# A two-block model on one core: weights stored in load order by the host, modulation sums moved from TensorE and GpSimd to VectorE and ScalarE, nine expert loads issued inside the first block

## The reference, cut to what matters

```python
# first block
h = rms_norm(x, norm1_g)
q, ckv, qi, ki, wi, u, v, ga, gb = split(h @ w_in)           # 1024 -> 4296 columns
index = sum_h wi_h * relu(qi_h @ ki.T)                       # 8 indexer heads
sel = top 64 of the causal index for each token
scores = q_lat @ c_kv.T * scale + rel_bias[bucket(t - s)]    # on the selected keys
o = softmax(scores) @ c_kv ; y_a = (o @ w_uv) @ w_proj_a
y_b = (gelu(u) * (tril(w_spatial) @ layer_norm(gelu(v)) + b_spatial)) @ w_proj_b
x = x + (sigmoid(ga) * y_a + sigmoid(gb) * y_b) @ w_out
x = x + moe(rms_norm(x, norm2_g))    # 32 experts, 2 for each token; three 1 MB matrices each
x = rms_norm(x, final_norm_g)
# second block, two layers
for l in range(2):
    mod = silu(c) @ w_ada[l] + b_ada[l]                      # (1024) @ (1024 x 3072)
    shift, scale, gate = split(mod)
    h = rms_norm(x) * (1 + scale) + shift
    x = x + gate * (concat(rglru_branch(h), mlstm_branch(h)) @ w_out[l])
return rms_norm(x, final_g)
```

## Time and profile before

| what | us |
|---|---|
| runs | 1045.84, 1049.13, 1050.15 (median 1049.13) |
| the profiled execution, its own time | 1043.84 |
| its span in the trace | 1042.0 |
| TensorE busy | 954.0 (92%) |
| VectorE, ScalarE, GpSimd busy | 423.5, 266.7, 178.3 |
| data moved | 227.86 MB, mean 219 GB/s |

### The profile page before, as it was taken

The page is one execution under the profiler, slowest core; times in us unless marked ns, Lnnn a source line. Parts: engine busy times, 40 slices in busy tenths (PEclk is TensorE's granted clock), DMA queues, the critical chain, the costliest instruction groups (busy, mean ns, idle before and its releaser), DMA issues.

```text
span 1042.0 us, 14265 instructions
## 1 busy us (share of the span) xinstructions
PE 954.0 (92%) x5525; PEld 758.9 (73%) x5525; DVE 423.5 (41%) x923; ACT 266.7 (26%) x623; POOL 178.3 (17%) x158
## 2 busy tenths in 40 slices
PE   6999799999899978666799999999999999999997
PEld 6868577788766644334388888787888888878786
DVE  1469862147622211110452453554325246264422
ACT  3231222201311211011218243133011814413301
POOL 5949997601100000000200000000000000000011
PEclk9999899989889997888899999999999999999999
DMA  9947776448999999999834554232354445423211
GB/s 290 284 160 242 232 207 194 162 152 298 421 420 422 420 421 421 421 420 420 287 108 155 162 161 143 101 122 77 126 162 122 159 144 162 162 88 115 99 43 41
DMA packets 140962, 227.86 MB, mean 219 GB/s; under 512 B 8457, under 2 KB 126562, under 8 KB 128602
## 3 DMA queue, kind: packets, MB, share of 16 engines
q1 hardware_dynamic: 136632, 221.15, 59.6%
q0 software_dynamic: 1600, 4.35, 1.6%
q10 hardware_dynamic: 2658, 1.40, 0.4%
HBM read 225.81 MB, written 1.07 MB: 218 GB/s over the span
## 4 chain that ended last, share of the span: by engine, by line
PE 74%; SPq 10%; DVE 8%; DMA 3%; issue 2%; ACT 2%; ACTq 0%; DVEq 0%
PE bank L469 25%; PE bank L1104 10%; SPq L1141 9%; PE bank L956 5%; PE bank L934 5%; PE bank L711 3%; PE bank L805 3%; PE bank L976 3%; DMA s<-in_w_down 3%; PE bank L781 2%; PE bank L820 2%; PE bank L452 1%; PE bank L841 1%; PE bank L521 1%; PE bank L991 1%
## 5 line engine op out<-in xcount | busy, mean ns | idle before, releaser
L469 PE MATMUL bank<-hT,ring 128*128 128x256 f32 x1168 | 264.0, 384 | 0.2 <-ACT s L1256 0.2
L469 PEld LDWEIGHTS bank<-hT,ring 128*128 128x128 f32 x1168 | 221.4, 192 | 35.6 <-issue 5.8
L1104 PE MATMUL bank<-ring,s 128*128 128x256 f32 x512 | 111.2, 379 | 0.0
L1104 PEld LDWEIGHTS bank<-ring,s 128*128 128x128 f32 x512 | 97.1, 190 | 13.1
L2214 POOL DMA_DIRECT2D s<-in_final_g x1 | 0.6, 604 | 472.8 <-DVE s L2057 472.8
L805 PE MATMUL bank<-s,z 128*32 128x256 f32 (+1 forms) x544 | 63.5, 415 | 8.8 <-DMA s<-in_w_up 6.4
L1832 DVE SCALAR_TENSOR_TENSOR z<-z,bank 128x256 f32<-128x256 f32 x9 | 3.8, 421 | 161.1 <-ACT z L1356 160.9
L2155 POOL TENSOR_TENSOR ring<-ring,csil 128x2048 f32<-128x2048 f32 x17 | 61.4, 3610 | 12.7 <-PE bank L495 11.7
L956 PE MATMUL bank<-ring,hT 128*128 128x256 f32 x256 | 56.6, 380 | 0.0
L934 PE MATMUL bank<-hT,ring 128*128 128x256 f32 x256 | 55.6, 379 | 0.0
L956 PEld LDWEIGHTS bank<-ring,hT 128*128 128x128 f32 x256 | 48.3, 190 | 7.7 <-issue 1.3
(11 more groups left out here) (413 smaller groups left out, 1490.9 us busy)
## 6 DMA issues: line engine op xcount, KB each, us to landing
ring<-in_w_in SPq DMA_DIRECT2D x56, 1024.0 KB, 5.4
ring<-in_w_ada SPq DMA_DIRECT2D x24, 1024.0 KB, 6.2
ring<-in_w_out SPq DMA_DIRECT2D x20, 1024.0 KB, 4.9
s<-in_w_gate SPq DMA_DIRECT2D x18, 1024.0 KB, 20.7
s<-in_w_up SPq DMA_DIRECT2D x16, 1024.0 KB, 22.1
ring<-in_w_down SPq DMA_DIRECT2D x12, 1024.0 KB, 23.6
s<-in_w_down SPq DMA_DIRECT2D x12, 1024.0 KB, 26.9
ring<-in_w_gate SPq DMA_DIRECT2D x10, 1024.0 KB, 25.6
```

What stands on the lines that cost most here:

```text
L469: mm = pe.matmul(b[:, 0:T], w[:, (k0 + kb) * CW + m * P:(k0 + kb) * CW + (m + 1) * P], rhs[:, kb, :], start=(kb == 0), stop=(kb == nk - 1))
L1104: mm = pe.matmul(xo[j, tt][:, 0:CW], yT[:, kb, tt * P:(tt + 1) * P], w[:, kb, :], start=(kh == 0 and kb == 0), stop=(kh == 1 and kb == KB ...
```

## The change

- The host now writes every piece of the two blocks in the order in which it is loaded, 8 KB for each partition, so a load is one contiguous 1 MB read. It also gives x turned (`x_T`), the small vectors as columns, the bias by distance and the spatial weights turned.
- `w_ada` pieces are stored with the output column on the partition and the 1024 inputs along the free axis, twice (two halves of 1024). One instruction with an accumulated output, 128x1024, does half a piece: VectorE does both halves of 18 pieces. For six pieces GpSimd does the 128x2048 multiplication alone, and ScalarE copies the two halves with accumulation. The 24 small TensorE jobs and the ScalarE copies of 2 columns go.
- The start: ScalarE and VectorE square x_T, TensorE sums over the partitions with a matrix of ones (8 matmuls, after 12 warming ones), ScalarE takes the root, VectorE the reciprocal of 128x256 and then writes the eight blocks of hT.
- The index weights come with the latent piece; the index key is written twice by two 64-column matmuls for each block. `cT` is turned between the two q pieces. The causal mask of the index is added by VectorE with `tri`.
- The bias of a head is added to the mask on VectorE ahead of the scores (`masked_bias`), and the matmuls with `anti` go. Two gate jobs stand ahead of the attention loop, and rounds 5 to 8 have one gate job instead of two.
- The biases of the spatial product are added on VectorE.
- Merged buffers: gmT in guT, oaT in w4, mgT in tga. So s6, s7 and vaug are dead in the whole first block. The first nine expert loads are issued behind pieces 14, 18, 22, 41 to 45 and 48; slots are used in another order.

The diff, cut to its core:

```diff
+GATES_FIRST, GATES_TWICE = 2, 5
+WARM_START = 12
-ADA_LAG = 2
-ADA_POOL = 17
+ADA_LAG = 1
+ADA_FIRST, ADA_POOL = 2, 6
+EARLY_LOADS = (14, 18, 22, 41, 42, 43, 44, 45, 48)
...
-        moe_slots = [RING + i for i in range(8)] + [(NB1 + i) % RING for i in range(RING)] + \
-            [RING + 8 + i for i in range(4)]
+        moe_slots = [RING + i for i in (7, 8, 6, 0, 2, 3, 1, 4, 5)] + [(NB1 + i) % RING for i in range(RING)] + \
+            [RING + i for i in (9, 10, 11)]
...
-                    for m in range(2):
-                        mm = pe.matmul(b[:, m:m + 1], adasum[:, n % 3, m * P:(m + 1) * P], allone[:, 0:1],
-                                       start=True, stop=True)
...
+            for _ in range(WARM_START):
+                pe.matmul(psum[0][:, 0:P], allone[:, :], allone[:, :], start=True, stop=True)
+            b = B.acquire(pe, "ssq")
             for kb in range(KB):
-                for tt in range(TT):
-                    m = pe.matmul(b[:, tt * P:(tt + 1) * P], x[:, tt, kb * P:(kb + 1) * P], rdiag[:, tt, :],
-                                  start=True, stop=True)
+                pe.wait_ge(S["sq_v" if kb // 2 % 2 else "sq_a"], 2 * (kb // 4) + kb % 2 + 1)
+                mm = pe.matmul(b[:, 0:T], allone[:, :], sqT[:, kb, :], start=(kb == 0), stop=(kb == KB - 1))
...
+            for _ in range(GATES_FIRST):
+                gate_job()
             for h in range(HEADS + 1):
...
-                        pe.matmul(b[:, 0:ns], anti[:, :], biasT[:, h, T - ns:T], start=True, stop=False)
...
-                gate_job()
+                if h < GATES_TWICE:
+                    gate_job()
...
-                    pe.matmul(b[:, c * P:(c + 1) * P], ones[0:1, :], bsp[0:1, g * P:(g + 1) * P], start=True, stop=False)
...
         def _(sp):
+            for n in range(NB1):
+                load(n, a["first_pieces"][n])
+                if n == RING - 1:
+                    sp.dma_start(x[:, :, :], ...)
+                if n in EARLY_LOADS:
+                    load_expert(len(early))
+                    early.append(n)
...
         def _(act):
+                if ADA_FIRST <= n < ADA_FIRST + ADA_POOL:
+                    act.wait_ge(S["ada_scaled"], n + 1 - ADA_FIRST)
+                    step(f(w[:, 0:D], w[:, 0:D], ACT.Copy, scale=0.5, accum_out=adac[:, l, 2 * j:2 * j + 1]))
+                    step(f(w[:, D:2 * D], w[:, D:2 * D], ACT.Copy, scale=0.5, accum_out=adac[:, l, 2 * j + 1:2 * j + 2]),
+                         S["ada_summed"])
...
         def _(v):
+            step(v.reciprocal(rbc, rbc))
+            for kb in range(KB):
+                step(stt(hT[:, kb, :], xT[:, kb, :], colA[:, kb:kb + 1], rbc, ALU.mult, ALU.mult), S["hT_ready"])
+            def ada_sums(count):
+                for n in range(ada["n"], ada["n"] + count):
+                    v.wait_ge(slot_full[c % RING], fill_value[c])
+                    step(stt(w[:, 0:D], w[:, 0:D], 0.5, csb, ALU.mult, ALU.mult, accum_out=adac[:, l, 2 * j:2 * j + 1]))
+                    step(stt(w[:, D:2 * D], w[:, D:2 * D], 0.5, csb, ALU.mult, ALU.mult,
+                             accum_out=adac[:, l, 2 * j + 1:2 * j + 2]), S["ada_summed_v"])
...
+            def masked_bias(h):
+                for tt in range(TT):
+                    step(tten(sc[:, tt, 0:ns], bias[:, h, T - ns:T], maskb[:, tt, 0:ns], ALU.add))
...
-                step(tten(gmT[:, g, :], b[:, 0:T], guT[:, g, :], ALU.mult), B.free)
+                step(tten(gsum, b[:, 0:T].rearrange("p (c t) -> p c t", c=TT),
+                          bsp[:, g, :].unsqueeze(1).broadcast_to([P, TT, P]), ALU.add))
+                step(tten(gmT[:, g, :], gsum.rearrange("p c t -> p (c t)"), guT[:, g, :], ALU.mult), B.free)
...
         def _(g):
-                    step(g.tensor_tensor(w, w, csil[:, :].unsqueeze(2).broadcast_to([P, KB, CW]), ALU.mult))
-                    step(g.tensor_tensor(w[:, 0:4, :], w[:, 0:4, :], w[:, 4:8, :], ALU.add))
-                    step(g.tensor_tensor(w[:, 0:2, :], w[:, 0:2, :], w[:, 2:4, :], ALU.add))
-                    step(g.tensor_tensor(adasum[:, n % 3, :], w[:, 0, :], w[:, 1, :], ALU.add), S["ada_summed"])
+                    step(g.tensor_tensor(w, w, csb.unsqueeze(1).broadcast_to([P, 2, D]), ALU.mult), S["ada_scaled"])
...
+def piece(w, tag):
+    if kind == "in":
+        t = by_column(w["w_in"][0], at[0])
...
+    elif kind == "ada":
+        l, j = at
+        t = w["w_ada_2"][l][:, j * CW:(j + 1) * CW].T.reshape(2, P, D).transpose(1, 0, 2)
```

562 lines of the change are left out of this document (233 added, 329 removed).

## The result

The changed kernel takes 1022.37 us, median of 4 runs (1020.47 to 1025.11), against 1049.62 for the kernel before (1045.84 to 1050.15): a ratio of 0.975 with a 95% interval of 0.972 to 0.978. It is faster, by 27 us where I forecast 49, and outside the range of 984 to 1019. The profiled execution took 1021.64 us, its span is 1019.9.

The account below looks back on a forecast made before the run. TensorE was taken to bound the first block, then the expert load stream; stage gains summing to 36.9 us put the experts at 254.6 and the last landing at 454.4, span 996.5, forecast 1000 us, range 984 to 1019.

Parts of the forecast that it names:

- q and index: Query and index stage: two modulation jobs go, gain 0.7 us; VectorE's wait cancels against the existing wait for the engines.
- rival D: First block: VectorE becomes the bound throughout, slower than before; 1060 at 9 us a modulation piece; chance 0.02.
- Rival B: Loads collide before the experts, TensorE waits for pieces, index stage may lose 5 to VectorE's start: 1018 us; chance 0.08.
- C: First block: fewer stalls than counted at V, the start's clock, q and index, and attention: 988 us; chance 0.17.
- Attention: Attention heads: bias matmuls and a job go (10.4 us), waits and slow clock too (8.1): gain 18.5.
- Start: Start to first qi projection: qi begins at 11.8 instead of 14.34, a gain of 2.5 us.
- cT, K, V: Small vectors, bias and cT: 4.6 us go, 2.5 come back through ScalarE's modulation copies ahead of K's: gain 2.1.
- Output projections: Output projections: four jobs go (1.4 us) and the first row runs at full clock (2.5).
- The stream: Expert loads: from the 19th issue at 258.4, 1.8 us start-up and 78 loads at 2.49; last lands at 454.4.
- the pairs of 64 columns side by side: Latent piece: doubled index-key matmuls of 64 columns run side by side at no cost; one after the other, 3.5 more.
- the spatial products: Spatial products: eight bias matmuls go (3.3 us), VectorE's second instruction shows with 0.7: gain 2.6.
- Rival A: VectorE's accumulating instruction runs at half pace, 4.7 us a modulation piece; experts begin 12 later: 1012 us; chance 0.15.

Follow-up runs that it names:

- e1: Changed kernel with each of GpSimd's six modulation multiplications shrunk to 8 of the 1024 columns of each half: 1010.64 us.
- e5: Changed kernel with GpSimd waiting for VectorE's last index sum before its first modulation multiplication, all work kept: 1018.07 us.
- e3: Changed kernel with ScalarE copying the previous head's transposed probabilities ahead of the two exponentials in attention rounds with one gate tile: 1016.87 us.
- e4: Changed kernel with ScalarE issuing the 512 KB broadcast load of c_2 only behind its squares: 1020.08 us.
- e10: Changed kernel with e3, e4, e6, all modulation sums on VectorE, seven throwaway matmuls before the first projection and x's load later: 1002.57 us.
- e6: Changed kernel with ScalarE's exponential of the recurrence parameters moved behind the copies of K and V: 1020.02 us.
- e11: Changed kernel with each of GpSimd's six modulation multiplications cut into four quarters of the columns: 1019.40 us.
- e7: Changed kernel with two more accumulating 128x1024 VectorE operations, results unread, in each of the eight attention rounds: 1023.54 us.

## Why the prediction was wrong

Its structure held: TensorE bounds the first block, the last landing hangs on the start of the experts, and 542 us follow. The last landing came at 477.7 instead of 454.4. Of these 23.3 us, 18.8 arose before the experts began (273.4 for 254.6), 0.4 up to the 19th load (4.2 for 3.85), and 4.1 in the stream (200.1 for 196.0).

The sum's step for the index stage failed first, with the largest miss:

- **q and index: "its wait should cancel" (7.5 us).** It did not cancel, and that is shown: e1 and e5 both bring the stage to 19.6, 10.5 below the changed kernel and 2.9 below even the forecast's 22.5. I had read the row in which a VectorE operation takes 3599 ns inside a multiplication, but used it only for VectorE's total load (rival D) and as 5 us in rivals B and C, not for the few small operations that stand ahead of the index on the path. That GpSimd keeps fewer pieces says nothing; when they run does. The one at 37.7 starts a quarter of a microsecond before the operation that all wait for.
- **Attention (4.8 of 18.5).** The round of 10 held. The late rounds took 7.83 and not 6.5, and not for VectorE, where I looked for it: ScalarE's order is worth 4.0 (e3, three waits), and the other 1.7 are a gate tile at the lower clock. With both gone e3 takes 80.1, less than the 81.0 of the forecast. The sum took TensorE's own work as the round. Whether the copy stands ahead of the exponentials was in the code.
- **Start (3.6).** x_T's second half landed 2.9 after the first, not 1.2; e4 shows half of that to be c_2's load. The sum over the partitions ended 1.6 behind the squares, not 0.5. The reciprocal took the 1.75 that I had given it. So qi began at 13.46 and not at 11.8, and it took 15.9 for 14.0 at a lower clock (0.90 in 13:30), of which throwaway work gives 1.0 back (e10).
- **cT, K, V (1.4).** I counted ScalarE's sums ahead of K's copies, not the exponential with its table load (e6).
- **Output projections (1.8).** The forecast's 2.5 for a full clock did not come, although the thin matmuls had gone: the first two rows took 2.67 and 2.94 us (clock 0.79 in 192:200) behind a wait of 2.46 for VectorE. That wait alone does not decide it: in e1, e4, e5, e6 and e11 it is the same, and the rows take 1.99 and 1.89. What does stays open.
- **The stream (4.1).** I took 78 loads at 2.49 and 1.8 of start-up from the 19th issue. The layer pieces are issued from 454.8, 23 us before the last `w_down` lands, and loads in flight share the engines, so some of their bytes go first. The bytes agree: at 417 GB/s these 200.1 us moved 83.4 MB, and 78 loads are 81.8; the 1.6 MB more are 3.8 us. The kernel before, too, issued layer pieces 23 us ahead of its last landing (from 476.55), so what I read there as 4 queued expert loads may in part have been these. No run separates it.
- **Right:** the pairs of 64 columns side by side, VectorE's 1.22 us for an accumulating 1024 columns, the spatial products, and 542 us at the end.

The rule weighed in the prediction, half pace for an accumulating two-input operation (the Trainium skill, "Vector Engine (DVE) Microarchitecture Reference", "Points that are easy to get wrong"), did not show: 1.22 us and 0.08 for the read in 33 of 36 operations, the pace of the row without accumulation; the other three took 1.62, each beside an addition of GpSimd. No rival named the time, and 1022.37 lies above the range. Rival A (1012) falls by the row at 48.91, and by e7 a second time. Of rival B (1018) the small part came true in another form, VectorE's late start in the index stage; the large one did not, as TensorE waits for no piece of w_out.

The sum's own target turned out to be reachable: e10, with these causes taken away, begins with the experts at 254.6, as the prediction said. That the two agree so closely is luck: e10 begins u at 57.85, where the sum has 63.1, and then takes 86.0 us for the attention, where the sum has 81.0. Its span is 1000.4 where 996.5 was forecast: the difference is the stream's.
